# Expert tiles of at most 64 rows computed with plain fp32 products in two column strips, in a mixture-of-experts stage on one Trainium2 core

## The reference, cut to what matters

```python
D_MODEL = 1024; N_EXPERTS = 8; TOP_K = 2; D_FF_E = 1408

def swiglu(h, w_gu, w_down):
    gate, up = jnp.split(h @ w_gu, 2, axis=-1)
    return (jax.nn.silu(gate) * up) @ w_down

def moe_swiglu(h, router_w, w_gu, w_down):
    probs = jax.nn.softmax((h @ router_w).astype(jnp.float32), axis=-1)
    top_p, top_i = lax.top_k(probs, TOP_K)
    top_p = top_p / jnp.sum(top_p, axis=-1, keepdims=True)
    gates = jnp.sum(jax.nn.one_hot(top_i, N_EXPERTS) * top_p[..., None], axis=-2)
    y = jnp.zeros_like(h)
    for e in range(N_EXPERTS):
        y = y + gates[..., e:e + 1] * swiglu(h, w_gu[e], w_down[e])
    return y
```

## Time and profile before

| | |
|---|---|
| median of 3 runs | 2010.56 us (2010.54 to 2017.06) |
| profiled execution, span from first to last instruction | 2009.5 us |
| expert stage (first fp32r product at 1262 us, last store at 1959 us) | about 697 us |
| TensorE busy in the span | 1909.8 us, 95% |

### The profile page before, as it was taken

One profiled execution on the slowest core, in us unless ns is written; L12 is line 12 of the kernel. 1 busy time (PEld: TensorE's weight loads), 2 busy tenths in 40 slices (PEclk: granted clock), 3 DMA queues, 4 the chain that ended last, 5 costly groups with the idle time before them and its releaser, 6 DMA issues. The chain is left out here.

```text
span 2009.5 us, 39776 instructions
## 1 busy us (share of the span) xinstructions
PE 1909.8 (95%) x14669; PEld 1550.9 (77%) x14670; DVE 1120.2 (56%) x1761; ACT 751.9 (37%) x1296; POOL 431.1 (21%) x360
## 2 busy tenths in 40 slices
PE   7899999999999999999999998999999999999995
PEld 5788888888886478887878776788887787787872
DVE  4676776677674644224222367665558558553347
ACT  4532442443331122221222102655547547553331
POOL 0245334435422222121121244100000000000003
PEclk9999999999999999999999999999999999999997
DMA  8234234224325353243222514976569669764354
GB/s 275 97 120 131 72 107 141 94 90 138 109 81 185 104 170 105 76 151 116 87 95 88 207 43 165 333 271 200 187 215 323 221 211 329 240 205 148 101 179 173
DMA packets 184794, 320.55 MB, mean 160 GB/s; under 512 B 26113, under 2 KB 77209, under 8 KB 184555
## 3 DMA queue, kind: packets, MB, share of 16 engines
q1 hardware_dynamic: 170283, 286.00, 42.9%
q0 software_dynamic: 8144, 28.84, 3.9%
q10 hardware_dynamic: 6128, 2.30, 0.4%
HBM read 284.41 MB, written 32.67 MB: 158 GB/s over the span
## 5 line engine op out<-in xcount | busy, mean ns | idle before, releaser
L1343 PE MATMUL pp<-whi,xTh 128*128 128x512 f32 (+1 forms) x1152 | 441.2, 383 | 13.6 <-issue 5.0
L2087 ACT ACTIVATE whi<-wring 128x1024 fp32r<-128x1024 f32 (+1 forms) x324 | 313.5, 979 | 343.7 <-PE pp L1345 293.6
L1344 PE MATMUL pp<-whi,xTl 128*128 128x512 f32 (+1 forms) x1152 | 430.0, 373 | 1.8 <-issue 1.8
L1345 PE MATMUL pp<-wlo,xTh 128*128 128x512 f32 (+1 forms) x1152 | 430.6, 374 | 0.0
L2736 DVE TENSOR_TENSOR wlo<-wring,whi 128x1024 fp32r<-128x1024 f32 (+1 forms) x180 | 209.5, 1164 | 191.6 <-ACT whi L2087 138.8
L1343 PEld LDWEIGHTS pp<-whi,xTh 128*128 128x128 f32 x1152 | 217.5, 189 | 54.0 <-issue 8.3
L1345 PEld LDWEIGHTS pp<-wlo,xTh 128*128 128x128 f32 x1152 | 217.6, 189 | 40.6 <-issue 2.2
L1344 PEld LDWEIGHTS pp<-whi,xTl 128*128 128x128 f32 x1152 | 217.9, 189 | 34.9
L1343 PE MATMUL pp<-whi,hTh 128*128 128x512 f32 x503 | 202.6, 403 | 5.3 <-DVE ybuf L2688 2.3
L2745 DVE TENSOR_TENSOR wlo<-wring,whi 128x1024 fp32r<-128x1024 f32 (+1 forms) x144 | 159.2, 1105 | 68.9 <-ACT whi L2087 59.2
L1345 PE MATMUL pp<-wlo,hTh 128*128 128x512 f32 x503 | 196.6, 391 | 0.0
(11 more groups left out here) (351 smaller groups left out, 3149.0 us busy)
## 6 DMA issues: line engine op xcount, KB each, us to landing
wring<-in_moe_w_gu SPq DMA_DIRECT2D x320, 256.0 KB, 4.2
wring<-in_ada_w SPq DMA_DIRECT2D x80, 512.0 KB, 4.8
wring<-in_moe_w_down SPq DMA_DIRECT2D x160, 256.0 KB, 3.8
wring<-in_ffn_w_gu SPq DMA_DIRECT2D x80, 256.0 KB, 2.9
wring<-in_dn_w_in SPq DMA_DIRECT2D x124, 128.0 KB, 2.9
wring<-in_ffn_w_down SPq DMA_DIRECT2D x40, 256.0 KB, 3.0
expert_in<-zeros SPq DMA_DIRECT2D x36, 256.0 KB, 3.3
wring<-in_ada_first SPq DMA_DIRECT2D x32, 256.0 KB, 6.2
```

Of the source, the lines that this page charges most:

```text
L1343: pe.matmul(out, hi[:, c0 + c, tt], wh, start=(first and c == 0), stop=False)
L1344: pe.matmul(out, lo[:, c0 + c, tt], wh, start=False, stop=False)
L1345: mm = pe.matmul(out, hi[:, c0 + c, tt], wl, start=False, stop=(last and c == nk - 1))
L2087: act.activation(whi[:, hs, 0:nk, 0:w], wring[:, ring_v.slot(k), 2 * s:2 * s + nk, 0:w], ACT.Copy)\
```

## The change

For each expert the last tile, when it holds at most 64 rows, is put first (its rows at 64 to 127 of the expert's tile 0), and every engine reads a flag `single` for it (row 2 of `tbl`). For such a tile TensorE does not use the three fp32r products: it multiplies plain fp32 tokens (64 columns stationary, `xT_raw`, `hT_raw`) with the raw fp32 weights of the ring. The output is in two column strips of the array: half of the columns goes to PSUM partitions 0 to 63, the other half to 64 to 127, 256 moving columns each (128 for the narrow halves). VectorE makes the raw copies of tokens and hidden values besides what it did before. All halves are still split to `whi` and `wlo`, for all experts.

Since TensorE now reads the raw weights, a ring place may be refilled only when TensorE is done with it. The ring is nine places of one half (`raw_halves`), and the fetch of half m waits on `slot_hi` of half m-5, which ACT makes only after TensorE has done half m-9. Code for three tiles and more is simplified (`OVER_ALL`): an expert that needs four is run as five.

```diff
-SLOTS = 18
+SLOTS = 21
+OVER_ALL = 3
+RAW = slice(4 * 128, 4 * 128 + 64)
+RAW_HALVES = 9
+        def raw_half(l, k, s):
+            return raw_halves[:, (2 * k + s) % RAW_HALVES, :, :] if l else wring[:, ring_of[0].slot(k), 2 * s:2 * s + 2, :]
...
+                def fill_halves(k, parts):
+                    if l == 0:
+                        return fill(k, parts, e, 18, l)
+                    for s in only:
+                        m = 2 * k + s
+                        if e or m >= RAW_HALVES:
+                            sp.wait_ge(S["slot_hi"], hi_count(1, m - RAW_HALVES + HALVES, e))
+                        for dst, src in parts(None)[s]:
+                            sp.dma_start(dst, src).then_inc(half_in(1, k, s), 16)
...
             moe_fill(0, 0)
+            moe_fill(0, 3)
+            moe_fill(0, 4, (0,))
...
+                        def strips():
+                            for c in range(nk):
+                                w = raw_half(1, k, s)[:, c, 0:width]
+                                for b in range(2):
+                                    if m < 24:
+                                        q = width // 4
+                                        dst = out[halves(b), 0:width].rearrange("p (g n) -> p g n", g=2)[:, :, q * b:q * b + q]
+                                        src = w.rearrange("p (g n) -> p g n", g=2)[:, :, q * b:q * b + q]
+                                        tokens = xT_raw[:, c0 + c, :]
+                                    else:
+                                        dst, src, tokens = out[halves(b), 0:256], w[:, 256 * b:256 * b + 256], hT_raw[:, c0 + c, :]
+                                    mm = pe.matmul(dst, tokens, src, start=(first and c == 0), stop=(last and c == nk - 1))
+                            mm.then_inc(done if last else f["half_done"], 1)
+                        if l and t == 0:
+                            with pe.If(single > 0):
+                                strips()
+                            with pe.Else():
+                                whole()
+                        else:
+                            whole()
...
-                def h_low(q0, n, j):
+                def h_low(q0, n, j, single=None):
                     nk = 2 if j < 5 else 1
+                    if l:
+                        with dve.If(single > 0):
+                            dve.wait_ge(f["hTh_ready"], q0 + 2)
+                            if nk == 2:
+                                dve.tensor_copy(hT_raw[:, 2 * j:2 * j + 2, :],
+                                                bank(7)[:, 0:3 * P].rearrange("p (k t) -> p k t", k=2)[:, :, 0:HB])
...
-            rts(dve.tensor_reduce(cnt[:, 0, 8:16], over, AX.X, ALU.add))
+            rts(dve.tensor_reduce(cnt[:, 0, 8:16], over[:, :, 0:T], AX.X, ALU.add))
+            rts(dve.tensor_reduce(cnt[:, 4, 8:16], over[:, :, T:2 * T], AX.X, ALU.add))
             rsync()
             rts(dve.tensor_tensor(cnt[:, 1, 8:24], cnt[:, 0, 7:23], cnt[:, 0, 6:22], ALU.add))
+            rts(dve.tensor_tensor(cnt[:, 6, 8:16], cnt[:, 0, 8:16], cnt[:, 4, 8:16], ALU.subtract))
             rsync()
+            rts(dve.scalar_tensor_tensor(tiles_before[:, 0, 4:4 + T, :], cnt[:, 6:7, 8:16].to_broadcast([P, T, 8]), float(HB),
+                                         tiles_before[:, 1, 4:4 + T, :], ALU.mult, ALU.add))
```

More of the change, by code:

```diff
@@ L731, in _ @@
                 sp.dma_start(norm_row(r), combo_dram[AG2 + r].partition_broadcast(P).rearrange("p (a n) -> p a n", a=2))\
-                    .then_inc(S["a2_in"], 16)
-            for k in range(2):
-                for split in slot_split:
-                    sp.wait_ge(split, k + 1 + 18 * 8 + 36)
-                for half in slot_loaded[ring.slot(k)]:
-                    sp.sem_inc(half, 32)
+                    .then_inc(S["end_rows"], 16)
+            for m in range(HALVES):
+                sp.wait_ge(S["slot_hi"], hi_count(1, m - RAW_HALVES + HALVES, 8))
+                sp.sem_inc(half_loaded[m], 32)
             ring.base += 2
@@ L1325, in nest, with half @@
                                 nest(n, body, t + 1)
-                def half(e, m, n, hi, lo, c0, bk, first, last, done, width, free, after=None, ahead=None):
+                def half(e, m, n, hi, lo, c0, bk, first, last, done, width, free, after=None, ahead=None, single=None):
                     k, s = m // 2, m % 2
@@ L1338, in tile @@
                             ahead(t)
-                        tt = slice(t * P, (t + 1) * P)
-                        for c in range(nk):
-                            wh, wl = whi[:, hs, c, 0:width], wlo[:, hs, c, 0:width]
-                            out = bank(bk(t))[:, 0:width]
-                            pe.matmul(out, hi[:, c0 + c, tt], wh, start=(first and c == 0), stop=False)
-                            pe.matmul(out, lo[:, c0 + c, tt], wh, start=False, stop=False)
-                            mm = pe.matmul(out, hi[:, c0 + c, tt], wl, start=False, stop=(last and c == nk - 1))
@@ L2807, in expert @@
                         if j:
[L2808 removed]
+                            h_low(c * 6 + n * (j - 1), n, j - 1, single)
                         if l:
```

270 lines of the change are left out of this document (171 added, 99 removed).

## The result

The changed kernel is slower: 2032.3 us (2027.1 to 2036.4, 4 runs) against 2013.3 us for the kernel before in the same comparison, ratio 1.009 with a 95% interval of 1.006 to 1.012. The forecast was 1963.5. The profiled execution took 2027.1 us, 1.5 us above its span; it is the fastest of the four, so spans stand 16 us apart where the medians stand 19.

What follows compares the result with a forecast made beforehand. TensorE, busy 1909.8 of 2009.5 us, was taken as the bound, with weights pacing one-tile experts. Terms -52.8 + 2.4 + 3 + 0.4 = -47 us gave a 1962.5 span, 1963.5 us median; range 1938 to 1994, about 0.8.

Steps and rivals of the forecast that it cites:

- The price of a product: Strips of experts 2, 6, 7: plain fp32 product of 256 columns at 0.223 us; 17.6 us saved an expert, -52.8 together.
- strips one after the other: Rival: strip pairs run in turn, a wide half saves only 0.11 us; 2008 us, no change; chance 0.06.
- Strips side by side: Two column strips of a half run at once: 0.225 us a row, 0.45 us a wide half.
- 0.35 us for the switch: Array shape change, there and back, in each half of flagged experts with two or more tiles: 0.35 us, bounds 0.20 to 0.60.
- The rival of exposed loads: 64-column loads not hidden behind their strip's products, 0.135 us a row, 1992 us; chance 0.09, shared with long branch stalls.
- Branches: A compare and an unconditional branch more each half: 1 us per one-tile expert, +3 us; bounds 0 and 21.
- the slower rival: TensorE's sequencer sets the pace through two extra branches in each of 288 halves: up to +53, 2063 us; chance 0.06.
- The weights set the pace: One-tile experts 0, 3, 5: 55 to 58 us, held by weight fetches at a DMA share of 0.95 to 0.96.
- Expert 5: One-tile expert taken as flagged: TensorE work falls from 45 to some 16 us, gain 0; bounds -2 and +2.
- The ring: Nine halves between frontiers instead of ten: 0.8 us lost in each one-tile expert, +2.4 us; bounds 0 and 4.6.
- Ahead of the experts: Packing chain gets three operations more, +0.4 us; the extra zeroing in the dense stage costs nothing.
- The tail: Part after the experts: not touched, no change forecast.

Runs made afterwards that it cites:

- The test alone: Kernel without strips, If and Else on the flag around tile 0 with the same products on both sides: 2037.6 us, against 2016.6 without the test.
- dead code: Kernel without strips plus a never-entered copy of a half's products in the part for four tiles: 2024.5 us, against 2016.6 without the copy.
- empty branches: Kernel without strips plus compare and branches ahead of tile 0 of every half, around only a register move: 2018.6 us, against 2016.6 without them.
- shorter code: Changed kernel, strips included, with the products of the fourth and fifth tile left out: 2006.0 us, against 2032.3 for the changed kernel.
- short code: Products of the fourth and fifth tile left out: 2007.9 us in the changed kernel without strips (2016.6 with them), 2001.3 in the kernel before.
- two loops: TensorE's expert loop twice, up to three tiles or full, chosen once: 2007.9 us for the change without strips, 2003.6 for the kernel before.
- the early release: Two-loop kernel without strips (2007.9), fetch of half m waiting only until half m-9 is split, not until m-5 is rounded: 1995.0 us, ratio 0.992.

## Why the prediction was wrong, point by point

**The price of a product: failed, and the gain with it.** The step was "Plain fp32 with 256 moving columns costs 0.223 us: sixteen in 3.72 us", and in the earlier trace rows "eight products of 512 fp32 columns". Sixteen and eight are records. The pooling mixer has 8 such products a tile in the program where the trace has 16 records, and the strips of the changed kernel 288 for 576. The source has four products at the line of the earlier trace rows too, for eight records. A product is two passes and costs 0.43 us. With that, a wide half in strips is 4 x 0.216 + 0.35 = 1.21 us, 0.15 less than 1.36, 30 of them 4.5 us; a narrow one gets 0.07 longer and a single row 0.10, together 0.5: 4.0 us an expert. The three experts measured 3.7, 4.1 and 3.4. So the strips gave 11.2 us in place of 52.8. The fp32r product of 512 columns is one record and 0.227 us, so three of them in a row of a half cost 0.68, two strips side by side 0.43: there was little more than a third to gain, and the switch took most of it. The rival "strips one after the other" gave 2.7 us an expert for another reason.

**Strips side by side, loads hidden, 0.35 us for the switch: right**, each with its rows above. The rival of exposed loads falls: the Trainium skill, "TensorE: Matmul & The Clock Gate", section "The mechanism", lets a load overlap a running product only where the row group differs. Here both strips use all rows, and rounds follow each other every 0.216 us, so by this trace the rule does not hold for strips.

**Branches: the place was right, the size not, and the cause was another.** The step that failed is the second one: 1 us for each one-tile expert, +3 us, with 21 as its upper bound. The test alone costs 21 us, 12 of them in these three experts, and in the changed kernel they lost 18.3. The forecast asked what an executed branch costs. What decided was the code that it jumps over, under a DMA share of 0.95: dead code alone cost 8 us, empty branches 2, and shorter code took 26 us off the changed kernel. The forecast's place for the slower rival, "both branches exposed at 0.22 in the 180 halves of unflagged experts", was wrong as well: expert 1 lost nothing, and the 18 us lie in experts 0, 3 and 5 in stalls of 1 to 4 us. "The weights set the pace" hid it: the one-tile experts waited partly for code, partly for permission to fetch, and the last 3 to 5% of the weights' bandwidth was not used.

**Expert 5: no strips at all.** The forecast, and the description of the change, take it for a flagged expert. It has 49 rows, but the marks for the flag begin at the second tile, so an expert with one tile never has it; the trace shows no strip product between 1672.3 and 1735.0. It lost 5.9 us, as experts 0 and 3 did, outside the bounds of 2; the forecast's 0 was its value for a flagged expert, so neither the size nor the reason held.

**The ring.** The forecast gave +2.4 us to the later release. With short code the one-tile experts of the ring of nine take 54.9, 53.8, 53.9, those of the old ring 54.0, 54.7, 55.0: nothing to choose; with two loops they are 55.9, 54.2, 54.8 and 53.9, 54.8, 54.9. What the early release shows is what looking further ahead is worth: 13 us for four halves more.

**Ahead of the experts.** Packing: from the first small product for the tile ranks (L1643, before L1548) to the first pick product it takes 6.0 us, and took 5.5; +0.5 for a forecast 0.4. From the first product of the dense stage to the first of the experts it takes 564.3 us and took 560.3; all versions of the change are 3.5 to 5.3 us longer there, the packing included, and the one with a far jump ahead of the stage 8.4. Nothing was forecast for the dense stage. One us of it is a wait that grew: TensorE's first product of the second dense expert waits 2.2 us for VectorE's `ybuf`, and waited 1.1 before. The rest, some 2 us and more, stays open: it is not the larger zeroing of the outputs, and the layout of memory and the code were not tried apart. **The tail** was forecast as untouched; with strips it is 2 to 4 us longer, from the last products on; why was not tested.

**The sum.** Between the forecast's change of span, -47 us, and the measured +16 lie 63 us: 42 from the price of a product (52.8 less 11.2), 13 from the one-tile experts (18.3 us lost where 3 + 2.4 was forecast), 3 ahead of the experts, 3 in expert 4 and 2 in the tail.

## What to carry to other kernels

Count program instructions against trace records before a duration becomes a price: one product can be two records. Where weights stream at a DMA share near 1 (0.95 here), the instructions come through the same engines (their queue has 0.5 to 0.7% of the 16 engines' time), so an alternative path of code can cost time even if nobody takes it. Look at the packets of the instruction queue and at branches over 1 us; keep rare cases out of the hot loop's body, in a second loop chosen once. And a DMA share of 0.95 still left 3 to 5% to gain: see first whether the fetches wait for permission.

## What the hardware showed that I had not expected

- A plain fp32 product of 256 columns is two records of 0.216 us each; an fp32r one of 512 columns is one of 0.227.
- Six products that are never run, added to each half, cost one-tile experts 2 to 4 us each; halving the bytes of the weights cut the cost of a test in each half from 21 us to 9.
- A branch over the code of a whole expert took up to 7.7 us.
- The core moved 355 to 357 GB/s at a DMA share of 0.99 to 1.00 when fetches could run thirteen halves ahead of TensorE, against 337 to 339 GB/s with nine.
